# Four edits in an MLA and short-convolution decode step: decode contexts folded in strips, last sums turned, first key head on VectorE, stores inside the last MLP group

## The reference, cut to what matters

```
h = rmsnorm(x); z = h @ w_in                      # latent, rope key, conv inputs
q, k, v = from the latents, 8 heads; k = rmsnorm([k_nope, rope(k_pe)])
prompt:  softmax(mask(q k^T)) v, causal
decode:  for each of 8 sequences: softmax(q k^T over 32 pages of 128 keys + 4 new keys) v
mix = [rmsnorm(attn), rmsnorm(gb * conv3(gc * hc))]
x = x + mix @ w_o
y = x + square(relu(rmsnorm(x) @ w_up)) @ w_down  # 1024 -> 4096 -> 1024, for 1056 tokens
outputs: y (1024 + 32 rows of 1024), latents, rope keys, conv states
```

## Time and profile before

| | us |
|---|---|
| median of 3 runs (lowest, highest) | 1985.18 (1984.08, 1985.4) |
| profiled execution | 1985.29 |
| its span in the profile | 1983.6 |
| PE busy, weight loads busy | 1904.1, 1801.8 |
| DVE, ACT, POOL busy | 949.6, 738.8, 455.9 |

### The profile page before, as it was taken

How to read it: one execution, slowest core, us unless ns; L and a number is a source line. 1 busy time by engine, 2 the same in 40 slices (tenths; PEclk the granted TensorE clock), 3 DMA queues, 4 the chain that set the end, 5 groups by cost and what they waited for, 6 DMA issues and landing times. The chain is left out here.

```text
span 1983.6 us, 36199 instructions
## 1 busy us (share of the span) xinstructions
PE 1904.1 (96%) x12672; PEld 1801.8 (91%) x12672; DVE 949.6 (48%) x1722; ACT 738.8 (37%) x1539; POOL 455.9 (23%) x434
## 2 busy tenths in 40 slices
PE   6999997999899999999998799999999999999998
PEld 5999996777689999999997599999999999999998
DVE  6115034777577777777776733322222222323132
ACT  5111123666566666666665332111111111111111
POOL 3242224333110000000000453222222312122221
PEclk8999998999999999999998699999999999999999
DMA  6122100000122222222231111021111112020202
GB/s 226 44 67 65 22 10 19 1 1 22 48 61 74 74 74 72 74 72 74 71 83 78 43 54 43 27 59 35 51 53 32 53 37 73 12 79 11 74 16 104
DMA packets 180605, 108.49 MB, mean 55 GB/s; under 512 B 52132, under 2 KB 177154, under 8 KB 180276
## 3 DMA queue, kind: packets, MB, share of 16 engines
q1 hardware_dynamic: 180358, 107.21, 19.0%
q10 hardware_dynamic: 174, 0.30, 0.1%
HBM read 97.47 MB, written 10.00 MB: 54 GB/s over the span
## 5 line engine op out<-in xcount | busy, mean ns | idle before, releaser
L2030 PE MATMUL banks<-comb_hi,pageT_hi 128*128 128x272 f32 x1024 | 233.8, 309 | 0.0
L1918 DVE TENSOR_REDUCE k_sums<-k_sq 128x8 f32<-128x512 f32 x256 | 174.3, 681 | 86.7 <-ACT k_sq L1746 86.5
L2030 PE MATMUL banks<-comb_hi,pageT_lo 128*128 128x272 f32 x1024 | 212.2, 289 | 0.0
L2030 PE MATMUL banks<-comb_lo,pageT_hi 128*128 128x272 f32 x1024 | 212.1, 288 | 0.0
L2394 DVE TENSOR_TENSOR xT<-xT,banks 128x1056 f32<-128x1056 f32 x64 | 80.3, 1254 | 272.8 <-PE banks L248 272.8
L1746 ACT ACTIVATE k_sq<-banks 128x512 f32<-128x512 f32 x256 | 152.0, 594 | 139.7 <-PE banks L2030 136.8
L2276 ACT ACTIVATE a_hi<-relu 128x1056 fp32r<-128x1056 f32 x32 | 34.9, 1090 | 386.6 <-DVE relu L2382 386.6
L237 POOL TENSOR_TENSOR w_down_lo<-w_down_raw,w_down_hi 128x512 fp32r<-128x512 f32 x64 | 94.7, 1479 | 339.8 <-ACT w_down_hi L233 339.8
L248 PE MATMUL banks<-a_lo,w_down_hi 128*128 128x352 f32 x768 | 166.7, 325 | 0.0
L248 PE MATMUL banks<-hf_hi,w_out_up_hi 128*128 128x352 f32 x768 | 166.3, 325 | 0.0
L248 PE MATMUL banks<-a_hi,w_down_lo 128*128 128x352 f32 x768 | 165.8, 324 | 0.0
(11 more groups left out here) (384 smaller groups left out, 3791.2 us busy)
## 6 DMA issues: line engine op xcount, KB each, us to landing
page_latents<-in_cache_kv_latent SPq DMA_DIRECT2D x256, 128.0 KB, 2.1
w_out_up_raw<-in_w_up SPq DMA_DIRECT2D x32, 512.0 KB, 4.7
w_down_raw<-in_w_down SPq DMA_DIRECT2D x64, 256.0 KB, 2.7
w_in_raw<-in_w_in SPq DMA_DIRECT2D x17, 512.0 KB, 3.9
x_spill<-xT SPq DMA_DIRECT2D x1, 4296.0 KB, 14.2
xT<-x_spill SPq DMA_DIRECT2D x1, 4296.0 KB, 13.7
page_ropes<-in_cache_k_rope SPq DMA_DIRECT2D x256, 16.0 KB, 1.8
w_out_up_raw<-in_w_o SPq DMA_DIRECT2D x8, 512.0 KB, 4.2
```

The costliest lines, as they stand in the source:

```text
L1918: nc.vector.tensor_reduce(ksum[par][:, j, :], sq[j % 2][:, :].rearrange("p (h c) -> p h c", h=H), AX_X, ALU.add)\
L2030: mm = pe.matmul(banks[:, 2 * (j % 2) + half, 0:WC], x[j % AHEAD][:, k, :], w[par][:, k, half, :], start=k == 0 and a == 0, stop=k == KL - ...
```

## The change

1. **Start of prompt attention.** DVE makes the key head 0 (both parts); POOL makes the query head 0 first and the constants behind it. PE waits for the constants behind the first 18 transposes.
2. **End of prompt attention.** ACT rounds `q_latent` before it keeps the last chunk of outputs. DVE no longer inverts the first chunk of the last pair's sums there.
3. **First decode group.** All three chunks of those sums are inverted by transposes, at pages 1 to 7, in place of five full reciprocals.
4. **End of decode attention.** Eight matmuls with 32 columns of `fold` add the strips of each sequence; four sequences stand over one another in the 128 partitions of a bank. One reciprocal (128x2) and one multiplication (128x512) follow, then 4 transposes.
5. **Stores.** The last MLP group is written out. Behind down product m (m over 0) PE turns feature tile m-1 of `xT` with 8 transposes into banks 6 and 7; ACT copies the first 512 tokens, DVE the others, into `y_tokens`. Tile 7 uses banks 1 and 2 and follows the last addition. SP stores in three pieces of columns (512, 256 and 256), 8 DMAs each, and two for the sampled rows. The phase `store_outputs` is gone.

```diff
-        for phase in (inputs, prompt_attention, sample_attention, output_and_mlp, store_outputs):
+        for phase in (inputs, prompt_attention, sample_attention, output_and_mlp):
...
                     prepare_q(0)
-                    prepare_k(0)
+                    constants()
+                    pool.wait_ge(s["k_head_ready"], 2)
                     prepare_q(1)
                     prepare_k(1)
...
+                    if is_head(n, H - 1) and go == GOES - 1:
+                        act.wait_ge(s["qab_copied"], KL)
+                        act.copy(g.qab_hi[:, :, :, :], g.qab[:, :, :, :]).then_inc(s["qab_split"], 1)
                 if is_head(n, H - 1):
                     keep_output(n, par, pair, 2)
-                    act.wait_ge(s["qab_copied"], KL)
-                    act.copy(g.qab_hi[:, :, :, :], g.qab[:, :, :, :]).then_inc(s["qab_split"], 1)
...
+            nc.vector.tensor_mul(kh[:, :, 0:NOPE], g.k_tok[:, :, 0:NOPE], scale(g.rkn, NOPE)).then_inc(s["k_head_ready"], 1)
+            nc.vector.tensor_mul(kh[:, :, NOPE:QK], g.kpe_tok[:, :, :], scale(g.rk, ROPE)).then_inc(s["k_head_ready"], 1)
...
                     latents_of_queries()
-                    invert_sums(pair, 0)
-                    invert_sums(pair, 1)
...
-            def invert_sums(x):
-                cols = slice(x * P, (x + 1) * P)
-                nc.vector.reciprocal(g.sums[:, cols], g.sums[:, cols]).then_inc(s["prompt_sums_inverted"], 1)
+            def invert_sums(c, back):
+                q0, q1 = g.sum_chunks[c]
...
+                if not back:
+                    nc.vector.transpose(turn.rearrange("p a b -> p (a b)"), sums).then_inc(s["prompt_sums_turned"], 1)
+                else:
...
-                        if j in (0, 1, 3, 5, 7):
-                            invert_sums((j + 1) // 2)
+                        if j in (1, 2, 3, 5, 6, 7):
+                            invert_sums(j // 3, j in (2, 5, 7))
...
-            nc.vector.tensor_mul(ctxs[:, :, 0:KVL], ctxs[:, :, 0:KVL], linv[:, :].unsqueeze(2).broadcast_to([P, NSEQ, KVL]))\
+            nc.vector.tensor_mul(ctxs[:, 0:2, 0:KVL], banks[:, 6:8, 0:KVL], linv[:, :].unsqueeze(2).broadcast_to([P, 2, KVL]))\
...
-            pe.matmul(banks[:, 2, 0:NSEQ], fold[:, :, :].rearrange("p a q -> p (a q)"), ctxs[:, :, KVL:KVL + 1].rearrange("p b o -> p (b o)"),
-                      start=True, stop=True).then_inc(s["sums_folded"], 1)
+            for a in range(2):
+                for r in range(QT):
+                    mm = pe.matmul(banks[r * HS:(r + 1) * HS, 6 + a, 0:KVL + 1], fold[:, 0, :], ctxs[:, a * QT + r, :], start=True, stop=True)
+            mm.then_inc(s["folded"], 1)
             pe.wait_ge(s["final_scaled"], 1)
             for k in range(KL):
-                for b in range(NSEQ):
-                    at = (k * NSEQ + b) * HS
-                    mm = pe.matmul(banks[:, 0, at:at + HS], ctxs[:, b, k * P:(k + 1) * P], fold[:, 0, :], start=True, stop=True)
+                for a in range(2):
+                    at = (k * 2 + a) * P
+                    mm = pe.transpose(banks[:, 0, at:at + P], ctxs[:, a, k * P:(k + 1) * P], ident[:, :])
...
+            for m0, m1 in PIECES:
+                cols = slice(m0 * P, m1 * P)
+                for half in range(2):
+                    sp.wait_ge(y_copied[half], m1)
+                    for t in range(half * HALF, half * HALF + HALF):
+                        sp.dma_start(A["out_y_prompt"][t * P:(t + 1) * P, cols], y[:, t, cols]).then_inc(y_stored, 16)
...
                     down.split_hi(act, m % 2, i * per + m // 2)
+                    if last and m > 1:
+                        keep_turned(m - 2)
+                if last:
+                    keep_turned(KD - 2)
+                    act.wait_ge(s_turned, 1)
+                    act.copy(y[0:NS, 2 * HALF, 0:BANK], banks[0:NS, S_BANK[0], :]).then_inc(s_copied[0], 1)
+                    keep_turned(KD - 1)
...
+                    if last and m > 0:
+                        turn_outputs(i, m - 1)
+                if last:
+                    turn_sampled(0)
+                    turn_outputs(i, KD - 1)
+                    turn_sampled(1)
```

More of the change, by code:

```diff
@@ L2221, in output_and_mlp, with y_bank @@
     turn = lambda i, f: KD // 2 + i * (FC // 2) + f // 2
+    HALF = SEQ // P // 2
+    S_BANK = (0, 6)
+    def y_bank(m, half):
+        return 6 + half if m < KD - 1 else 1 + half
+    PIECES = ((0, 4), (4, 6), (6, KD))
+    y_turned = [sem(f"y_turned_{n}") for n in ("low", "high")]
+    y_copied = [sem(f"y_copied_{n}") for n in ("low", "high")]
+    s_copied = [sem(f"y_sampled_copied_{n}") for n in ("low", "high")]
+    s_turned, y_stored = sem("y_sampled_turned"), sem("y_stored")
     with nc.Block() as block:
@@ L2228, in _, with group @@
                 sp.dma_start(ring.raw[m % 2][:, :, :], w_o[:, :, m * P:(m + 1) * P]).then_inc(ring.loaded[m % 2], 16)
-            with sp.Fori(0, GROUPS) as i:
+            def group(i):
                 for f in range(FC):
@@ L2242, in _ @@
                         .then_inc(down.loaded[s], 16)
+            with sp.Fori(0, GROUPS) as i:
+                group(i)
+            for m0, m1 in PIECES:
[4 more added lines that the diff above has]
+                        sp.dma_start(A["out_y_prompt"][t * P:(t + 1) * P, cols], y[:, t, cols]).then_inc(y_stored, 16)
+            for part in range(2):
+                cols = slice(part * BANK, (part + 1) * BANK)
+                sp.wait_ge(s_copied[part], 1)
+                sp.dma_start(A["out_y_sample"][:, cols], y[0:NS, 2 * HALF, cols]).then_inc(y_stored, 16)
+            sp.wait_ge(y_stored, 16 * (2 * HALF * len(PIECES) + 2))
         @block.scalar
@@ L2263, in _, with group @@
             norm.act_inverse(act)
-            def group(i, first):
+            def group(i, first, last=False):
                 if not first:
@@ L2354, in group, with turn_outputs, turn_sampled @@
                                   lambda k: a_hi[:, k, :], lambda k: a_lo[:, k, :], first=hidden)
+                    if last and m > 0:
[4 more added lines that the diff above has]
+                    turn_sampled(1)
+            def turn_outputs(i, m):
+                pe.wait_ge(down.evacuated[m % 2], i * per + m // 2 + 2)
+                for half in range(2):
+                    if 0 < m < KD - 1:
+                        pe.wait_ge(y_copied[half], m)
+                    for x in range(HALF):
+                        at = META + (half * HALF + x) * P
+                        mm = pe.transpose(banks[:, y_bank(m, half), x * P:(x + 1) * P], xT[:, m, at:at + P], g.ident[:, :])
+                    mm.then_inc(y_turned[half], 1)
+            def turn_sampled(part):
+                if part == 1:
+                    pe.wait_ge(y_copied[0], KD - 1)
+                for x in range(KD // 2):
+                    mm = pe.transpose(banks[0:NS, S_BANK[part], x * P:(x + 1) * P], xT[:, part * (KD // 2) + x, TP:T], g.ident[:, :])
+                mm.then_inc(s_turned, 1)
             group(0, True)
-            with pe.Fori(1, GROUPS) as i:
+            with pe.Fori(1, GROUPS - 1) as i:
                 group(i, False)
+            group(GROUPS - 1, False, True)
         @block.vector
@@ L2377, in _, with keep_turned, group @@
             inv = blocked(norm.inv[:, :])
-            with v.Fori(0, GROUPS) as i:
+            def keep_turned(m):
+                v.wait_ge(y_turned[1], m + 1)
+                nc.vector.tensor_copy(y[:, HALF:2 * HALF, m * P:(m + 1) * P],
+                                      banks[:, y_bank(m, 1), :].rearrange("p (a b) -> p a b", b=P)).then_inc(y_copied[1], 1)
+            def group(i, last=False):
                 for f in range(FC):
@@ L2446 @@
+                    if last and m > 0:
+                        keep_turned(m - 1)
+                if last:
+                    keep_turned(KD - 1)
+                    v.wait_ge(s_turned, 2)
+                    nc.vector.tensor_copy(y[0:NS, 2 * HALF, BANK:D], banks[0:NS, S_BANK[1], :]).then_inc(s_copied[1], 1)
+            with v.Fori(0, GROUPS - 1) as i:
+                group(i)
+            group(GROUPS - 1, True)
 _OUTS = [("y_prompt", (SEQ, D)), ("y_sample", (NS, D)), ("new_lat_prompt", (TP, KVL)), ("new_kpe_prompt", (TP, ROPE)),
```

90 lines of the change are left out of this document (34 added, 56 removed).

## The result

| | before | after |
|---|---|---|
| median of 4 runs (lowest, highest), us | 1985.29 (1984.08, 1986.88) | 1973.92 (1972.28, 1976.04) |
| profiled execution; its span | 1985.29; 1983.6 | 1974.61; 1972.8 |

The account below looks back on a forecast made before the run. PE's own stream was taken to bound the kernel, with gains only where PE stands still. Terms 0.85 + 2.2 - 0.9 + 6.2 + 2.0 = 10.4 us off 1985.29 gave 1974.9, median 1974.8; range 1971 to 1978.3.

Parts of the forecast that it names:

- Start of prompt attention: POOL's query head, with the constants behind it, starts earlier and PE's transposes follow: gain 0.85 us, bounds 0 and 0.85.
- The keys' own estimate of 1.2 us: Start of prompt attention: DVE makes the first key head in 1.2 us, ready near 338.3, before the queries at 338.55.
- the lower bound of 0 ("should DVE be the later one"): Start of prompt attention: no gain if DVE's keys were ready later than POOL's queries.
- End of prompt attention: ACT's cast ends earlier and DVE's low part is last, so both end together: gain 2.2 us, bounds 0 and 2.2.
- First decode group: A reciprocal and a transpose back delay DVE's masked scores at page 4: PE loses 0.87 us, bounds 0 and 1.1.
- the first rival, "the clock stays up": End of prompt attention: PE's 3.66 us gap is too short for the clock to fall; total 1973.3 us; chance 25%.
- End of decode attention: Fold, division and 4 transposes take 4.73 us in place of 10.93, the fold 1.94 of it: gain 6.2 us.
- The estimate by the Trainium skill's factor, 2.8 us: End of decode attention: fold time by the skill's 3.07 times for four packed tiles; the sum would be 0.9 us less.
- the 8.5 us: End of decode attention: fold time if strips run one after another, 16 unpacked matmuls at half clock 0.53 us each.
- Stores: 48 transposes cost 5.4 us, the tail takes 9.85 in place of 17.29: gain 2.0 us, bounds -0.9 and 5.7.
- the rival of lockstep: Last MLP group: ACT's cast waits for the turned tile, so products wait and it ends slower; within a 4% chance.
- the DMAs eating the gain: Stores: 26 DMAs in place of 9 land 2 us later, making the stores' term 0; total 1976.8 us; chance 15%.

Follow-up runs that it names:

- keys_behind_queries: Changed kernel with VectorE's first key head waiting for POOL's first query head; 1972.93 us in one run.
- after_again: The changed kernel run once more, unchanged; median 1975.79 us, ratio to the kernel before 0.9954.
- only_sums: Kernel before with only items 2 and 3 of the change (the sums at the end of prompt attention and first decode group); ratio 0.9985.
- fold_pairs: Changed kernel with the 8 folding matmuls reordered so that two neighbours share a strip; 1981.24 us in one run.

## Why the prediction was right, step by step

- **Start of prompt attention: mis-sized, 0.85 us said, 0.26 measured.** The step "the query head starts 0.85 us earlier" was right, and the silent step behind it, that POOL's query head still takes 1.65 us and ends at 338.55, was wrong: with DVE's two products beside it it took 2.27, which takes 0.62 of the 0.85 us away. The keys' own estimate of 1.2 us was right for DVE by itself (1.22 us in `keys_behind_queries`, from 339.16 to 340.38) and wrong beside POOL (2.57), but PE never waited for them, so the lower bound of 0 ("should DVE be the later one") held for another cause than the one it names.
- **End of prompt attention: right,** 2.21 us; ACT and DVE ended within 0.03 us of each other, as reckoned.
- **First decode group: right in mechanism,** 0.75 us more wait where 0.87 was said. That the net was only 0.06 was luck: in this profile the stretch at half clock gave 0.69 back, the first rival, "the clock stays up", in part. It was 3.4 us long in place of 6.8, but `after_again` has 6.8 us over the same gap and a net loss of 1.09. The Trainium skill's warning of idle gaps ("TensorE: Matmul & The Clock Gate", section "Why this matters for your kernels"), by which the clock would not stay up over the gap, agrees with the trace: it fell at 541.4, 0.3 us behind the gap of 3.66.
- **End of decode attention: right,** 6.18 us; the fold took the 1.94 us of the row of the same shape, strips and clock. The estimate by the Trainium skill's factor, 2.8 us, was off by 0.9. Part of that lies in the 8.5 us to which the factor was put: 4.4 times from four strips suggests that the price of the unpacked matmul, taken from another shape, was too high.
- **Stores: right,** 5.23 and 9.82 us against 5.4 and 9.85, 2.2 us gained where 2.0 was said. No wait of PE stands in the last group, so the rival of lockstep fell, and so did the DMAs eating the gain; but the ten last issues were a bound that the sum had at 0.45 us each (0.47 measured) and took for given. Merging them and splitting the last piece was worth 2.0 us more.
- **Outside the sum:** -1.61 us in the inputs (variation) and +1.55 in the MLP (a half-clock stretch that comes with this schedule). They cancel; either alone would have put the forecast off by 1.6 us, inside its range. Inside the sum the start brought 0.6 us less than was said and the first decode group lost 0.8 less, which cancel in the same way. That the total came within 1 us is luck, since one kernel's executions differ by more than that (1972.28 to 1976.04); that it lies in the range is not.

## What to carry to other kernels

Take the price of an operation that moves beside another engine's from a row in which the two run together; DVE and POOL on SBUF operands took turns here. In a kernel bound by PE, read each wait with the granted clock behind it, and in more than one execution, since the same wait was followed by 0, 6.8 or 20.4 us at half clock. Transposes that nobody reads, sized to end before the other engines, took 4.1 us off the end of decode attention. And judge a part worth 2 us by its place in the timeline: its time alone, with 10 runs, could not tell it from nothing.

## What the runs showed of the hardware that was not expected

- Half clock under a fully busy PE: 20.4 us from 520.0 in `only_sums` and from 521.0 in `fold_pairs`, 1.5 and 1.6 us behind the end of a wait of 1.5 us, where other profiles have 6.8 us behind the same wait or, as `after_again`, none.
- The contention slows POOL's small operations too: in `keys_behind_queries`, where DVE's products ran beside them, its mask took 0.65 us and its cast 0.50, in place of 0.29 each.
- In the window of 3 us shown above, DMAs of 128 KB issued 0.47 us apart moved 266 GB/s from SBUF to HBM, and DMAs of 512 KB with rows of the same length moved 338.
